# The skipped branch of a mixture of experts, moved from behind the last pair of experts to a place between the ninth and the tenth

## The reference

```
for l in range(2):
    h = modulate(rms_norm(x, norm1_g[l]), sh1, sc1);  x = x + g1 * token_mixer(h, ...)
    h = modulate(rms_norm(x, norm2_g[l]), sh2, sc2);  x = x + g2 * hier_moe(h, ...)
# hier_moe: a router gives every token 2 of 32 experts and their gates
hu = lax.ragged_dot(xs, w1, sizes)                  # xs: tokens sorted by expert
h_gate, h_up = jnp.split(hu, 2, axis=-1)
ys = lax.ragged_dot(jax.nn.silu(h_gate) * h_up, w2, sizes)
out = jnp.zeros_like(t).at[tok_s].add(ys * gate)
```

## Time and profile before

| | us |
|---|---|
| median of 3 runs | 2311.27 |
| profiled execution | 2302.7 |
| its span | 2300.9 |
| PE busy | 2134.7 (93%) |
| DVE busy | 963.1 (42%) |
| ACT busy | 685.9 (30%) |
| POOL busy | 284.1 (12%) |

### The profile page before, as it was taken

How to read it: one execution, slowest core, us unless ns; L and a number is a source line. 1 busy time by engine, 2 the same in 40 slices (tenths; PEclk the granted TensorE clock), 3 DMA queues, 4 the chain that set the end, 5 groups by cost and what they waited for, 6 DMA issues and landing times.

```text
span 2300.9 us, 30193 instructions
## 1 busy us (share of the span) xinstructions
PE 2134.7 (93%) x12867; PEld 1500.7 (65%) x12867; DVE 963.1 (42%) x1892; ACT 685.9 (30%) x1224; POOL 284.1 (12%) x145
## 2 busy tenths in 40 slices
PE   6999888999999989998899999999998899998998
PEld 4787674555544567777645555554774699978997
DVE  2466632212111136566312221221245577756776
ACT  3434421101101034353211110110203555555554
POOL 4554420000000034554000000000000000000000
PEclk8999989999999989999899999999999999998999
DMA  9965669999999976657689999999355375334651
GB/s 347 325 226 206 242 241 380 409 409 409 409 409 409 408 275 224 220 220 293 271 347 389 409 409 409 409 409 404 126 206 213 130 235 187 109 115 167 199 173 48
DMA packets 242742, 657.30 MB, mean 286 GB/s; under 512 B 12923, under 2 KB 116837, under 8 KB 230184
## 3 DMA queue, kind: packets, MB, share of 16 engines
q1 hardware_dynamic: 239936, 651.74, 74.8%
q0 software_dynamic: 1184, 2.08, 0.3%
q10 hardware_dynamic: 1480, 1.45, 0.2%
HBM read 654.17 MB, written 1.06 MB: 285 GB/s over the span
## 4 chain that ended last, share of the span: by engine, by line
PE 86%; DVE 10%; ACT 3%; issue 1%; DMA 0%; POOL 0%; ACTq 0%; DVEq 0%
PE ps L410 85%; DVE AR L1971 2%; DVE AR L747 1%; DVE AR L2018 1%; PE ps L2648 0%; DVE ARr L1646 0%; DVE AR L1231 0%; ACT AR L818 0%; ACT AR L2621 0%; ACT HBr L387 0%; PE ps L2472 0%; DMA hT<-in_onehot 0%; DVE ringr L393 0%; DVE AR L1114 0%; ACT hTr L827 0%
## 5 line engine op out<-in xcount | busy, mean ns | idle before, releaser
L410 PE MATMUL ps<-ring,AR 128*64 128x512 f32 (+2 forms) x2016 | 514.7, 577 | 31.4 <-DVE AR L2018 31.4
L410 PE MATMUL ps<-XLr,HBr 128*128 128x256 f32 x1280 | 375.5, 293 | 22.1 <-DVE ringr L393 6.9
L410 PE MATMUL ps<-AR 128*128 128x128 f32 (+6 forms) x2088 | 380.9, 345 | 14.0 <-DVE AR L1952 7.5
L410 PEld LDWEIGHTS ps<-ring,AR 128*64 128x64 f32 (+1 forms) x2016 | 196.8, 140 | 268.9 <-issue 264.0
L410 PEld LDWEIGHTS ps<-AR 128*128 128x128 f32 (+2 forms) x2088 | 290.0, 192 | 119.5 <-issue 76.4
L410 PE MATMUL ps<-hTr,ringr 128*128 128x256 f32 x1280 | 366.5, 286 | 0.0
L410 PE MATMUL ps<-hTr,HBr 128*128 128x256 f32 x1280 | 366.2, 286 | 0.0
L393 POOL TENSOR_TENSOR ringr<-ring,HBr 128x1024 fp32r<-128x1024 f32 x110 | 266.3, 2436 | 777.6 <-ACT HBr L387 777.4
L387 ACT ACTIVATE HBr<-ring 128x1024 fp32r<-128x1024 f32 x260 | 266.3, 1050 | 196.6 <-PE ps L410 179.9
L410 PEld LDWEIGHTS ps<-XLr,HBr 128*128 128x128 f32 x1280 | 249.4, 195 | 43.6 <-issue 24.8
L410 PEld LDWEIGHTS ps<-hTr,ringr 128*128 128x128 f32 x1280 | 250.2, 195 | 2.1 <-issue 1.0
(11 more groups left out here) (311 smaller groups left out, 2593.9 us busy)
## 6 DMA issues: line engine op xcount, KB each, us to landing
ring<-in_w_expert_in SPq DMA_DIRECT2D x155, 1024.0 KB, 14.8
ring<-in_w_expert_out SPq DMA_DIRECT2D x81, 1024.0 KB, 11.0
ring<-in_mod_w SPq DMA_DIRECT2D x48, 1024.0 KB, 6.6
ring<-in_ffn_w_up SPq DMA_DIRECT2D x44, 1024.0 KB, 5.2
ring<-in_w_in SPq DMA_DIRECT2D x40, 1024.0 KB, 5.6
ring<-in_w_ada SPq DMA_DIRECT2D x40, 1024.0 KB, 8.2
HB<-in_w_expert_in SPq DMA_DIRECT2D x35, 1024.0 KB, 14.6
HB<-in_w_expert_out SPq DMA_DIRECT2D x23, 1024.0 KB, 12.3
```

The source lines that it names most:

```text
L410: return pe.op.matmul(out_, lhsT, rhs, start=start, stop=stop, **kw)
```

## The change

The four branches are moved up in both layers: OVER_AT is 9, and each engine's test and body now stand ahead of pair 9. On SP they stand ahead of that pair's loads. On PE scatter(8) is done ahead of the branch, and so ahead of up(9) and no longer behind it; the other scatters stay. Within the body two waits name pair 8 where they named pair 15, and PE's body waits for the copies of gather(9).

```diff
@@ sp_moe
             for p in range(NE // 2):
+                if p == OVER_AT:
+                    sp_over(sp, l, W1, W2)
                 for which, W, parts in (("w1", W1, 4), ("w2", W2, 2)):
...
+        OVER_AT = 9
+
+        def sp_over(sp, l, W1, W2):
             sp.wait_ge(*dve_moe["flag", l])
             flag = sp.op.value_load(ints[0:1, l * 16 + 15:l * 16 + 16], min_val=0, max_val=8)
             with sp.op.If(flag > 0):
...
-                    part.wait_ge(*(pe_over[l]["scatter", j - 1] if j else pe_moe["scatter", l, 15]))
+                    part.wait_ge(*(pe_over[l]["scatter", j - 1] if j else pe_moe["scatter", l, OVER_AT - 1]))
@@ pe_moe_all
             for p in range(NE // 2):
+                if p == OVER_AT:
+                    pe_scatter(pe, l, m, p - 1)
+                    pe.wait_ge(*dve_moe["flag", l])
+                    flag = pe.op.value_load(ints[0:1, l * 16 + 15:l * 16 + 16], min_val=0, max_val=8)
+                    with pe.op.If(flag > 0):
+                        pe_over_all(pe.part(), l, m)
                 pe_up(pe, l, m, p)
-                if p:
+                if p and p != OVER_AT:
                     pe_scatter(pe, l, m, p - 1)
...
             pe_scatter(pe, l, m, NE // 2 - 1)
-            pe.wait_ge(*dve_moe["flag", l])
-            flag = pe.op.value_load(ints[0:1, l * 16 + 15:l * 16 + 16], min_val=0, max_val=8)
-            with pe.op.If(flag > 0):
-                pe_over_all(pe.part(), l, m)
@@ act_moe_all, and dve_moe_all in the same way
             for p in range(NE // 2):
+                if p == OVER_AT:
+                    act.wait_ge(*dve_moe["flag", l])
+                    flag = act.op.value_load(ints[0:1, l * 16 + 15:l * 16 + 16], min_val=0, max_val=8)
+                    with act.op.If(flag > 0):
+                        act_over_all(act.part(), l, m)
                 act_up(act, l, m, p)
...
-            act.wait_ge(*dve_moe["flag", l])
-            flag = act.op.value_load(ints[0:1, l * 16 + 15:l * 16 + 16], min_val=0, max_val=8)
-            with act.op.If(flag > 0):
-                act_over_all(act.part(), l, m)
@@ dve_over_all
-            dve.wait_ge(*pe_moe["scatter", l, NE // 2 - 1])
+            dve.wait_ge(*pe_moe["scatter", l, OVER_AT - 1])
@@ pe_over_all
+            pe.wait_ge(*act_moe["GT", l, OVER_AT])
+            pe.wait_ge(*dve_moe["xg", l, OVER_AT])
```

More of the change, by code:

```diff
@@ L2112, in dve_moe_all @@
             for p in range(NE // 2):
+                if p == OVER_AT:
+                    dve.wait_ge(*dve_moe["flag", l])
+                    flag = dve.op.value_load(ints[0:1, l * 16 + 15:l * 16 + 16], min_val=0, max_val=8)
+                    with dve.op.If(flag > 0):
+                        dve_over_all(dve.part(), l, m)
                 dve_up(dve, l, m, p)
@@ L2119, in dve_moe_all @@
                     normC.dve(dve)
[L2120 to L2123, removed]
             g2 = mods[:, l * 48 + 40:l * 48 + 48]
```

## The result

The changed kernel takes 2323.15 us (median of 16 runs, 2312.96 to 2326.4), the kernel before 2312.71 us (16 runs, 2306.36 to 2318.2). The ratio is 1.0051 with a 95% interval of 1.0042 to 1.0060.

The account below looks back on a forecast made before the run. PE's order of instructions was taken to bound the experts, the weight stream close behind. Added 20.7 us less 8.8 removed gave 11.9 us; on a median of 2311.3 that forecast 2323 us, range 2311 to 2333.

Parts of the forecast that it names:

- (a): Ahead of scatter(8), now directly behind down(8): PE waits 0.91 us per layer for both copies of y(8), 1.8 us.
- (b): Between scatter(8) and up(9): PE idles at the branch as at the ends, 3.63 + 3.44 = 7.1 us.
- Rival 1: Branch costs PE nothing in the middle, test passed during scatter(8): 2308 to 2313 us; chance 0.12.
- (c): In up(9), behind the branch: the clock falls to half, 1.7 us per layer, 3.4 us (0 to 3.4).
- (d): Ahead of gather(10): scatter(8) no longer covers DVE's P(10), so PE waits 3.03 us per layer, 6.1 us.
- (e): In gather(10), behind its gap: half clock costs 1.7 us per fall, two of three, 2.3 us (0 to 3.4).
- a sign of being right: Per layer, the tanhs of pairs 8 and 10 lie 9 to 11 us further apart than those of 6 and 8.
- Ends: Time removed at the experts' ends: 3.7 us in layer 0, 5.1 in layer 1; together 8.8 (6.0 to 10.7).
- The gap of 3.44 and the fall of the clock behind it: Removed behind layer 1's last scatter: 3.44 us idle and 1.68 of slow clock, 5.1 us (3.4 to 5.1).
- Net: Whole kernel: 20.7 us added less 8.8 removed, 11.9 us slower.
- Engines beside PE at nothing: ACT's, DVE's and SP's moved branches cost nothing: idle stretches of 13.1 and 13.7 us, SP's lead of fourteen us.
- Rivals 2 and 3: Second: SP's test starves PE of weights, 2331 us, chance 0.06. Third: dearer fetch or smaller return, up to 2331, 0.13.

Follow-up runs that it names:

- e2: The changed kernel without its four branches and bodies, leaving only scatter(8) ahead of up(9): 2317.26 us, 1.0027 of the kernel before.
- e6: The changed kernel with all four tests and jumps kept but bodies of a single wait: 2317.02 us, 1.0036 of the kernel before.
- e7: The changed kernel with a body of one round in place of seven: 2316.19 us, 1.0041 of the kernel before.
- e9: The kernel before, branches at their old place, with bodies of a single wait: 2300.2 us, 0.9964 of the kernel before.
- e3: The changed kernel with DVE building P and G of pair 10 ahead of its work on h(9): 2312.27 us, 1.0001 of the kernel before.
- e5: The changed kernel run once more, unaltered, beside three other kernels: 2322.06 us, 1.0061 of the kernel before.
- e8: The changed kernel with SP's branch alone put back behind the next stage's first loads: 2325.12 us, 1.0067 of the kernel before.
- e10: The changed kernel with P and G of every pair built one step earlier: 2302.2 us, 0.9957 of the kernel before.
- e1: The kernel before without its four branches and their bodies in both layers: 2298.51 us, 0.9950 of the kernel before.

## Why the prediction was right

The forecast of 2323 us met the median, and the net of 11.9 us lies within what was measured: 10.4 us by the medians, 9.7 to 13.9 by the ends of the ratio's interval (0.0042 and 0.0060 times 2312.7). That it met it to 0.2 us is luck: the net is 1.5 above the medians' difference, and the kernel before was taken 1.4 too low, at 2311.3. The mechanism was right, a gap at every place that was named. By its steps, for the two layers of the profiled execution:

- *(a) wait for y(8)*: 1.8 predicted, 2 x 0.88 measured. Right, though the order as a whole costs 1.3 us per layer there (e2): 0.4 of it is not in the gap, and no term had it.
- *(b) branch in the middle*: 7.1 predicted, 3.47 + 3.20 = 6.7 measured. The size was right, presumably since the same scatter stands ahead of it in both places. Its reading was too coarse: "from the load of the flag to the first instruction behind the body" is really only the fetch, as e6, e7 and e9 showed. Rival 1 was thus right on the test and wrong on the fetch.
- *(c) the clock behind it*: 3.4 predicted; 40.30 - 35.06 - 3.47 = 1.8 and 39.96 - 35.06 - 3.20 = 1.7, so 3.5. Right for this execution; over the ten such places of after, e3, e5, e8 and e10 it lies between 1.4 and 3.1.
- *(d) P's lost cover*: 6.1 predicted, 3.06 + 3.07 measured, and e3 took all of it away. Pair 0 had shown it beforehand in the kernel before.
- *(e) the clock behind that*: 2.3 predicted as an average over falls; 3.0 in layer 0 and 0.1 in layer 1, so 3.1. The bound of 1.7 per fall was too low: e2 shows 2.8 and 3.0. With it pairs 8 to 10 of layer 0 became longer by 12.6 us, where 9 to 11 had been named as a sign of being right; layer 1 has 9.3.
- *Ends*: layer 0 3.7 predicted, 4.2 measured. Layer 1 5.1 predicted, 3.7 measured; the step "The gap of 3.44 and the fall of the clock behind it" was mis-sized, the clock fell one multiplication later, which stood there as the lower bound. By e1 the whole branch is worth 12 us (6 to 17), against 8.8 predicted; e1's profile shows 9.5 of it and the changed kernel's 7.9, and whether more than the spread of the clock is in the difference stays open.
- *Net*: 11.9 predicted, 14.0 by the places of the profile, 10.4 by the medians. The last stages, which the sum didn't touch, took 7.7 us more in the changed kernel's profile; how much of that is in the medians is not known.
- *Engines beside PE at nothing*: right for SP (e8). ACT's and DVE's idle time ahead of up(9) swallowed their branches; DVE waited for the tanh at each milestone. Rivals 2 and 3 didn't come: PE named no slot, and the gap in the middle was no dearer than at the end.

## What to carry to other kernels

A branch that skips a long body cost the time to fetch what lies behind it here, 3.2 to 4.0 us, and not the test. Keep the body short, or put the branch where the engine has several microseconds of issued work that waits for nothing: the end of the 7.1 us of down(15) hid it, the 3.7 us of a scatter that waits for another engine's result didn't. When a step is moved out of its place, ask what it was covering there: here the small scatter covered DVE's matrices, and the loss of that cover cost 9.2 us in the two layers, nearly as much as the branch in the middle (10.1) and far more than the wait for y(8).

## What the runs showed beside

Equal gaps don't cost equal clock. The gap of 3.06 us ahead of gather(10) was followed by a gather of 3.84 to 6.79 us in the twelve cases of six profiles; gaps in the last stages, the same in every kernel, add 7 to 8 us in one execution and not in another. From pair 1 to 2 of layer 1 it is 38.84 us in the kernel before and the changed one, but 43.06 in e3's profile and 44.70 in e6's, which alter nothing in that pair. A change worth 5 us on PE can be lost in that spread, and a single pair of profiles misjudged this one by a factor of two.
